# Two transformer blocks with experts on one core: overflow code laid aside, first routing and tail reordered, shorter reciprocal root

## The chip, the core and the metric

The kernel is one program on one core of a Trainium2 chip. The metric is device time in microseconds (us), the median of three runs. Its engines are TensorE (PE), VectorE (DVE), ScalarE (ACT), GpSimd (POOL) and SyncE (SP), each with its own queue of instructions; they wait for one another on semaphores.

## The reference, cut

All tensors are fp32. There are 256 tokens (272 with 16 meta tokens in the first block) of width 1024. The first block has two layers with mixers (a recurrent RG-LRU, then gated linear attention), a layer norm behind each mixer and each feed-forward part, and in its second layer a choice of 2 of 8 experts (width 3584). The second block has a modulated norm, attention, and 2 of 4 experts in the best of 4 groups (16 experts, width 512).

```
h = layer_norm(alpha * h + gla_block(h), g1, b1)              # "ln2" in the kernel
top_w = softmax(top_k(h @ router, 2))                         # routing 1, 8 experts
y = sum_e gates[:, e] * (silu(h @ w_gate[e]) * (h @ w_up[e])) @ w_out[e]
h = layer_norm(alpha * h + y, g2, b2)[16:]                    # "ln3"
x = h + g1 * attention(modulate(rms(h)))                      # the middle
gate = hierarchical top-2 of 16 of x7 = modulate(rms(x))      # routing 2
out = x + g2 * sum_e gate[:, e] * (silu(x7 @ w_g[e]) * (x7 @ w_u[e])) @ w_d[e]
```

## The kernel before

A value that enters a product is split into a high and a low part. In the mixers, the dense feed-forward part and the middle, weights come as a stream `M` of chunks: SyncE loads `raw`, ScalarE makes the high part `whi` (`split_hi`), VectorE the low part `wlo` (`split_lo`), TensorE uses both. For the first chunk of the middle GpSimd makes `wlo` (`pool_split_lo`), and GpSimd also ends the norm `ln3` (`pool_ln`).

*First expert layer.* VectorE's `dve_route1` takes the two largest logits of each token (`dve_top2`), their shares and gates (`dve_top2_gates`) and one-hot `masks`. TensorE multiplies these into counts and ranks. `dve_places` sorts the eight experts by their counts into a list `perm`, which SyncE reads to issue the weights' transfers (`load_first`, a ring R1 of 11 slots of 1.05 MB), and computes for every token its place in its experts' groups (`of_place`) and a flag, whether an expert has more tokens than its pair has room for. The experts work in four pairs, rank x with rank 7-x, in `pe_first`, `act_first` and `dve_first`: `choose` writes the selection matrices `sel`, `choose_sel` turns them, `part` gathers the tokens, `up`, `down` and `scatter` follow. Before `choose(0)`, VectorE also ends the norm `ln2` (`dve_ln_finish`) and makes the tokens' low parts `hl`.

*Overflow.* After each expert layer every engine waits for the others' `round_m1` or `round_m2`, reads the flag from memory and branches over the code of the overflow rounds that stands there in an `If` (`first_again`, `pairs_again`). In the given data the flags are zero. SyncE's output (`sp_out`) stands before its own second `If`.

*The middle.* ScalarE spreads the gate of the attention branch over the partitions (`act_spread`), VectorE and ScalarE make the rms norm, with `gc`, the product of gain and modulation. Reciprocal roots are `dve_rsqrt`: an initial value from the bits and three Newton steps, eleven dependent steps in all.

*Second expert layer.* Eight pairs in `pe_pairs`, `act_pairs` and `dve_pairs`, weights in a ring R2 of 13 slots, issued by `load_ring`. The scattered results of all pairs add up in four banks (Y, `ps0` to `ps3`); the result of a down product lies in two D banks. ScalarE copies a D bank times the token's gate to `yh`, VectorE makes the rest `yl`, TensorE scatters both one pair later. Behind the last scatter VectorE multiplies Y by the modulation's gate `g2t` and adds the residual `h`. The order on each engine is the one the code is written in; no scheduler changes it.

## Time and profile before

| | before |
|---|---|
| median of three runs | 1953.35 us (1952.22 to 1957.31) |
| profiled execution, its own time | 1952.21 us |
| its span | 1950.3 us |
| mean granted TensorE clock | 0.962 |
| busy: PE, DVE, ACT, POOL | 1803.6, 609.2, 474.7, 356.6 us |
| read from memory | 579.96 MB |

Busy time is the time in which an engine works on an instruction; register, branch and semaphore instructions don't count. The stages in order are: the first block up to routing 1 (to about 626 us), the first expert layer (to 1498), the middle (to 1709), the second expert layer (to about 1936) and the end. An idle time is given in square brackets with the instruction that ended it.

### The profile page before, as it was taken

What the parts mean: (1) busy time and instruction counts of PE and PEld (TensorE: products, weight loads), DVE (VectorE), ACT (ScalarE), POOL (GpSimd) and SP (SyncE); (2) the same over time, 40 slices, a digit from 0 to 9 for tenths busy, and PEclk for the clock granted to TensorE, in tenths of its full rate; (3) what the DMA queues carried; (4) which work ended last, traced back from release to release, by engine and by line L of the source; (5) the groups of instructions that cost most, each with busy time, mean ns of one, the idle gap of its engine ahead of it and who ended that gap; (6) DMA issues with size and microseconds to landing.
All of it is one profiled execution on the core that took longest, in us unless ns stands there. A gap on an engine that the chain in (4) does not pass through costs nothing.

```text
span 1950.3 us, 26935 instructions
## 1 busy us (share of the span) xinstructions
PE 1803.6 (92%) x11133; PEld 1026.3 (53%) x11133; DVE 609.2 (31%) x1248; ACT 474.7 (24%) x797; POOL 356.6 (18%) x307
## 2 busy tenths in 40 slices
PE   8999999999987899999999999999996887699996
PEld 7987999777965333323332333223232786544442
DVE  6777555338475200100010000000002686500111
ACT  5854434325421110000100000001001564322120
POOL 3000000000000699999920000000000201000000
PEclk9998999998998799999999999999998898799998
DMA  6545666447625999999999999999995640589995
GB/s 191 157 136 200 199 206 216 152 131 249 195 87 196 395 400 386 420 420 420 416 420 420 420 416 418 420 420 419 418 419 218 181 134 31 216 321 420 419 419 232
DMA packets 152744, 582.93 MB, mean 299 GB/s; under 512 B 11673, under 2 KB 77866, under 8 KB 109600
## 3 DMA queue, kind: packets, MB, share of 16 engines
q1 hardware_dynamic: 150000, 575.09, 75.8%
q0 software_dynamic: 2608, 5.97, 1.2%
q8 instruction: 93, 1.52, 0.3%
q14 instruction: 43, 0.35, 0.1%
HBM read 579.96 MB, written 1.05 MB: 298 GB/s over the span
## 4 chain that ended last, share of the span: by engine, by line
PE 44%; DMA 14%; DVE 6%; ACT 2%; issue 1%; DVEq 0%; SPq 0%; ACTq 0%
PE ps L1765 16%; DMA ring<-in_moe_w_out 10%; PE ps L2200 6%; PE ps L1758 4%; PE ps L1797 4%; PE ps L2224 3%; DMA ring<-in_moe_w_in 3%; PE ps L1801 1%; DMA more<-in_moe_w_in 1%; PE ps L2167 1%; PE ps L2185 1%; PE ps L436 1%; PE ps L2168 1%; PE ps L438 1%; PE ps L437 1%
## 5 line engine op out<-in xcount | busy, mean ns | idle before, releaser
L1765 PE MATMUL ps<-ring,xg 128*64 128x512 f32 x1638 | 407.2, 600 | 5.5 <-DMA ring<-in_moe_w_in 2.6
L472 DVE TENSOR_TENSOR wlo<-raw,whi 128x2048 fp32r<-128x2048 f32 (+5 forms) x96 | 211.5, 2206 | 190.6 <-ACT whi L464 190.3
L1765 PEld LDWEIGHTS ps<-ring,xg 128*64 128x64 f32 x1638 | 121.4, 137 | 249.1 <-issue 239.9
L464 ACT ACTIVATE whi<-raw 128x2048 fp32r<-128x2048 f32 (+6 forms) x97 | 178.8, 1846 | 187.2 <-PE ps L438 70.9
L436 PE MATMUL ps<-xh,whi 128*128 128x272 f32 (+1 forms) x712 | 210.4, 295 | 1.2 <-DVE xl L521 1.2
L438 PE MATMUL ps<-xh,wlo 128*128 128x272 f32 (+1 forms) x712 | 208.5, 293 | 0.0
L1797 PE MATMUL ps<-ring,ahm 128*64 128x512 f32 x808 | 202.9, 597 | 5.9 <-DMA ring<-in_moe_w_out 5.8
L437 PE MATMUL ps<-xl,whi 128*128 128x272 f32 (+1 forms) x712 | 208.3, 293 | 0.0
L2133 POOL TENSOR_SCALAR lnt<-lnt,h 128x384 f32<-128x384 f32 x120 | 188.5, 1571 | 12.2
L1935 DVE TENSOR_TENSOR sgm<-sgm,ps 128x512 f32<-128x512 f32 x28 | 17.4, 682 | 501.1 <-PE ps L1765 501.1
L742 POOL DMA_DIRECT2D lnt<-in_ln_gain x4 | 2.2, 559 | 799.7 <-issue 513.8
L436 PEld LDWEIGHTS ps<-xh,whi 128*128 128x128 f32 (+1 forms) x712 | 133.5, 188 | 4.5 <-issue 2.4
L437 PEld LDWEIGHTS ps<-xl,whi 128*128 128x128 f32 (+1 forms) x712 | 133.7, 188 | 0.4
L438 PEld LDWEIGHTS ps<-xh,wlo 128*128 128x128 f32 (+1 forms) x712 | 133.3, 187 | 0.5
L1797 PEld LDWEIGHTS ps<-ring,ahm 128*64 128x64 f32 x808 | 63.3, 136 | 129.0 <-issue 129.0
L2135 POOL TENSOR_TENSOR bias<-bias,lnt 128x384 f32<-128x384 f32 x120 | 120.2, 1002 | 10.0
L436 PE MATMUL ps<-whi,xh 128*128 128x256 f32 (+3 forms) x368 | 111.7, 304 | 4.2 <-DVE wlo L472 2.0
L437 PE MATMUL ps<-wlo,xh 128*128 128x256 f32 (+3 forms) x368 | 110.6, 301 | 0.0
L438 PE MATMUL ps<-whi,xl 128*128 128x256 f32 (+3 forms) x368 | 110.3, 300 | 0.0
L1758 PE MATMUL ps<-ring,xg 128*32 128x384 f32 (+1 forms) x936 | 106.6, 554 | 2.1 <-DMA ring<-in_moe_w_in 1.9
L2200 PE MATMUL ps<-ring,xg 128*64 128x512 f32 x392 | 99.3, 604 | 1.6 <-ACT xg L2265 1.6
L1945 DVE SCALAR_TENSOR_TENSOR yl<-ps,gs,yh 128x512 fp32r<-128x512 f32 x8 | 5.6, 747 | 265.3 <-ACT yh L1883 265.3
(581 smaller groups left out, 2422.9 us busy)
## 6 DMA issues: line engine op xcount, KB each, us to landing
ring<-in_moe_w_in SPq DMA_DIRECT2D x117, 1024.0 KB, 19.6
ring<-in_moe_w_out SPq DMA_DIRECT2D x101, 1024.0 KB, 19.9
ring<-in_moe_w_in SPq DMA_DIRECT2D x117, 768.0 KB, 11.8
ring<-in_w_gate SPq DMA_DIRECT2D x29, 1024.0 KB, 13.6
raw<-in_ffn_w_in SPq DMA_DIRECT2D x28, 1024.0 KB
ring<-in_w_down SPq DMA_DIRECT2D x26, 1024.0 KB, 13.0
raw<-in_w_ada SPq DMA_DIRECT2D x24, 1024.0 KB
ring<-in_w_up SPq DMA_DIRECT2D x20, 1024.0 KB, 11.9
```

The lines of the kernel that those rows point to most:

```text
L436: e.matmul(o, lh, rh, start=start, stop=False)
L437: e.matmul(o, lh, rl, start=False, stop=False)
L438: return e.matmul(o, ll, rh, start=False, stop=stop)
L464: e.activation(whi[0:rows, s % NSPL, 0:n], raw[0:rows, i % NRAW, 0:n], ACT.Copy).then_inc(S.hi.s, S.hi.up((s,)))
L472: e.tensor_tensor(wlo[0:rows, s % NSPL, 0:n], raw[0:rows, i % NRAW, 0:n], whi[0:rows, s % NSPL, 0:n].bitcast(F32), ALU.subtract).then_inc( ...
L1758: ins = e.matmul(po[32 * c:32 * c + 32, 0:n // 4], a[:, j, 128:160], quarter(both[0][:, 0, :], n, c), start=j == 0, stop=j == 7)
L1765: ins = e.matmul(ps_[b][64 * v:64 * v + 64, :], a[:, j, 64 * v:64 * v + 64], both[v][:, 0, 512 * b:512 * b + 512], start=j == 0, stop=j == 7)
L1797: ins = e.matmul(D[q][64 * v:64 * v + 64, :], w["ahm"][:, f, 64 * v:64 * v + 64], both[v][:, i, 512 * q:512 * q + 512], start=f == 0, stop ...
L2133: e.tensor_scalar(stp[:, :], rel[:, :], float(th), dl[:, i, hh:hh + 1], ALU.is_ge, ALU.mult).then_inc(pool.s, pool.up())
L2135: e.tensor_tensor(bias[:, hh, :], bias[:, hh, :], stp[:, :], ALU.add).then_inc(pool.s, pool.up())
L2200: ins = e.matmul(p[64 * v:64 * v + 64, :], xg[:, kk_, u + 64 * v:u + 64 * v + 64], both[v][:, k, :], start=kk_ == 0, stop=kk_ == 7)
L2224: ins = e.matmul(D[q][64 * v:64 * v + 64, :], w["ah"][:, x % 2, f, 64 * v:64 * v + 64], both[v][:, i, 512 * q:512 * q + 512], start=f == 0 ...
```

## The change

- `dve_rsqrt` keeps three Newton steps, but half of the value is folded into the first two instructions and each step runs on y and x*y*y/2 in two dependent instructions: eight dependent steps.
- Overflow: each compute engine has the overflow rounds' code ahead of its main program (`aside`), jumped over at the start. The flag is loaded into a register earlier (`load_flag`: at step 20 of the first pair of layer 1, and in the second layer at a step of the fifth pair), and at the old place a compare-and-branch (`ask`) falls through where the flag is zero. SyncE has a block of its own for each layer (`sp_first_again`, `sp_pairs_again`), the second now before the output.
- The first chunks of the middle are issued each when the slot of R1 that it overlays is read for the last time (`last_in`), and the parameters of the norms as soon as their buffer is free.
- Routing 1: the masks come before the shares, the counts get a product of their own ahead of the ranks', the sort is `dve_order`, the expert of rank x is paired with the one of rank 4+x (the step `back` goes), the norm's ending and `hh`/`hl` are done per tile, the gather of tile 0 comes before `choose_sel(0)`, and the second tile's part, the shares and the flag (`dve_route1_end`) stand between `choose(0)` and `choose(1)`.
- Start of the middle: the first chunk's low part is made by VectorE in two halves (`split_half`), one before and one after the mean square; ScalarE makes two high parts before its squares.
- Routing 2: masks before the shares.
- Second layer: VectorE multiplies D by gate and `g2t` into `z`, which gives back the D bank; ScalarE copies `z` to `yh`, VectorE makes `yl = z - yh`; the last pair has buffers of its own (`yh7`, `yl7`). The residual is added by a product of the identity with `h` into Y at `scatter(2)`; `scatter(6)` stands behind `down(7)`; the result is copied out of Y half by ScalarE and half by VectorE, and each tile goes out by itself.

```diff
+    def split_half(e, S, s, half):
+        i = S.split[s]
+        a = slice(CW // 2 * half, CW // 2 * half + CW // 2)
+        e.wait_ge(S.hi.s, S.hi.at(s))
+        ins = e.tensor_tensor(wlo[:, s % NSPL, a], raw[:, i % NRAW, a], whi[:, s % NSPL, a].bitcast(F32), ALU.subtract)
+        if half:
+            ins.then_inc(S.lo.s, S.lo.up((s,)))
+        else:
+            ins.then_inc(dve.s, dve.up())
...
+        for i in range(begin, end):
             _, rows, n, pieces, s, zero = S.chunks[i]
             k = i % NRAW
+            if first <= i < first + NRAW:
+                e.wait_ge(pe.s, pe.at("ring", R1.name, last_in(ring[:, 2 * NSPL + k, :])))
             if i >= NRAW:
...
         e.wait_ge(dve.s, dve.n)
-        e.tensor_scalar(y.bitcast(I32), x.bitcast(I32), 1, None, ALU.logical_shift_right).then_inc(dve.s, dve.up())
-        e.wait_ge(dve.s, dve.n)
-        e.tensor_scalar(y.bitcast(I32), y.bitcast(I32), -1.0, 1597463007.0, ALU.mult, ALU.add).then_inc(dve.s, dve.up())
-        e.tensor_scalar(x, x, -0.5, None, ALU.mult).then_inc(dve.s, dve.up())
-        for _ in range(3):
+        e.tensor_scalar(y.bitcast(I32), x.bitcast(I32), -0.5, 1597463007.0, ALU.mult, ALU.add).then_inc(dve.s, dve.up())
+        e.wait_ge(dve.s, dve.n)
+        e.scalar_tensor_tensor(x, y, 0.5, x, ALU.mult, ALU.mult).then_inc(dve.s, dve.up())
+        for i in range(3):
             e.wait_ge(dve.s, dve.n)
-            e.tensor_tensor(tmp, y, y, ALU.mult).then_inc(dve.s, dve.up())
+            e.scalar_tensor_tensor(tmp, x, -1.0, y, ALU.mult, ALU.mult).then_inc(dve.s, dve.up())
             e.wait_ge(dve.s, dve.n)
-            e.tensor_tensor(tmp, tmp, x, ALU.mult).then_inc(dve.s, dve.up())
-            e.wait_ge(dve.s, dve.n)
-            ins = e.scalar_tensor_tensor(y, tmp, 1.5, y, ALU.add, ALU.mult)
-            ins.then_inc(dve.s, dve.up())
+            if i < 2:
+                e.scalar_tensor_tensor(x, tmp, 1.5, x, ALU.add, ALU.mult).then_inc(dve.s, dve.up())
+            e.scalar_tensor_tensor(y, tmp, 1.5, y, ALU.add, ALU.mult).then_inc(dve.s, dve.up())
...
+    def dve_places(e):
+        p = bank("rank", 8)
+        e.wait_ge(pe.s, pe.at("rank", 8))
+        e.tensor_copy(w1["rk"][:, :, 0:8], p[:, 0:32].rearrange("p (t n) -> p t n", t=2)[:, :, 0:8]).then_inc(dve.s, dve.up(("flag", 8)))
+        pick_out(e, of_place[:, 1], masks[:, :, 0:8], 2)
+        pick_out(e, of_place[:, 0], w1["rk"][:, :, 0:8], 2)
         dve.label(("places",))
-        pick_out(back.unsqueeze(1), many.unsqueeze(1), 1)
...
             sel = w["sel"][:, x % 2]
             p, pg = bk.take(e, key, "sel", x), bk.take(e, key, "gs", x)
             e.wait_ge(C.dve.s, C.dve.at(key, "sel", x))
-            e.wait_ge(dve.s, dve.at("places"))
...
 
-        choose_sel(0)
+        e.wait_ge(dve.s, dve.at("m1", "hl"))
+        e.wait_ge(C.dve.s, C.dve.at(key, "sel", 0))
         for i in range(4):
             part(0, i)
+        choose_sel(0)
...
+            return
+        root[engine] = nc.cur_bb
+        e.br(f"{engine}_main")
+        for n, body in bodies:
+            with nc.body(f"{engine}_again{n}", valid_engines=[e.engine]):
+                body(e, engine)
+                e.br(f"{engine}_past{n}")
+        nc.switch_bb(f"{engine}_main")
...
+        e.br_ne(flag[engine, n], 0, on_true=f"{engine}_again{n}", on_false=f"{engine}_past{n}")
+        nc.switch_bb(f"{engine}_past{n}", parent=root[engine])
 
...
         e.wait_ge(dve.s, dve.n)
         e.tensor_copy(tw[:, :, 0:2], gi[:, :, 0:2]).then_inc(dve.s, dve.up())
         e.tensor_tensor(tw[:, :, 2:3], gw[:, :, 41:42], gw[:, :, 40:41], ALU.subtract).then_inc(dve.s, dve.up((key, "gap")))
+        e.wait_ge(dve.s, dve.n)
+        for t in range(2):
+            e.tensor_scalar(masks[:, t, 0:n], io, tw[:, t, 0:1], None, ALU.is_equal).then_inc(dve.s, dve.up())
+            e.tensor_scalar(other[:, t, 0:n], io, tw[:, t, 1:2], None, ALU.is_equal).then_inc(dve.s, dve.up())
...
+        e.wait_ge(dve.s, dve.at("ln2", "full", 0))
+        act_moe_parts(e, "m1", lambda t: w1["hh"][:, t, :], lambda t: h[:, t, :], (0,))
         act_ada(e, 5)
-        e.wait_ge(dve.s, dve.at("ln2", "full"))
-        act_moe_parts(e, "m1", lambda t: w1["hh"][:, t, :], lambda t: h[:, t, :])
+        e.wait_ge(dve.s, dve.at("ln2", "full", 1))
+        act_moe_parts(e, "m1", lambda t: w1["hh"][:, t, :], lambda t: h[:, t, :], (1,))
...
+        e.tensor_scalar(far[:, :], cst[:, C_IO:C_IO + 128], 256.0, None, ALU.add).then_inc(dve.s, dve.up())
+        dve_ln_finish(e, "ln2", 2, XTILES[:1])
         e.wait_ge(pe.s, pe.at("m1", "logits"))
         e.tensor_copy(gw[:, :, 0:8], logits("m1", 8)).then_inc(dve.s, dve.up(("m1", "logits")))
         dve_top2(e, "m1", 0, 8)
+        dve_moe_parts(e, "m1", lambda t: w1["hh"][:, t, :], lambda t: w1["hl"][:, t, :], lambda t: h[:, t, :], (0,))
+        dve_order(e)
+        dve_places(e)
+        e.wait_ge(dve.s, dve.n)
+
+    def dve_route1_end(e):
+        dve_ln_finish(e, "ln2", 2, XTILES[1:])
+        dve_top2_share(e, "m1")
         dve_top2_gates(e, "m1", 8)
-        dve_places(e)
+        dve_moe_parts(e, "m1", lambda t: w1["hh"][:, t, :], lambda t: w1["hl"][:, t, :], lambda t: h[:, t, :], (1,))
+        pick_out(e, of_place[:, 2], gates[:, :, 0:8], 2)
+        dve.label(("gates", "of place"))
         dve_ada(e, 5)
-        dve_ln_finish(e, "ln2", 2, XTILES)
-        e.wait_ge(dve.s, dve.n)
-        dve_moe_parts(e, "m1", lambda t: w1["hh"][:, t, :], lambda t: w1["hl"][:, t, :], lambda t: h[:, t, :])
+        dve_over(e)
 
...
         def scatter(x):
+            if x == 2:
+                for t in range(2):
+                    for q in range(2):
+                        e.matmul(Y[t, q][:, :], idn, h[:, t, 512 * q:512 * q + 512], start=False, stop=False)
             e.wait_ge(C.dve.s, C.dve.at(key, "yl", x, 1))
             for t in range(2):
                 for q in range(2):
-                    for n in ("yh", "yl"):
-                        ins = e.matmul(Y[t, q][:, :], w["selT"][:, x % 3, t, :], w[n][:, 512 * q:512 * q + 512],
-                                       start=(x == 0 and n == "yh"), stop=(x == NP - 1 and n == "yl"))
-            ins.then_inc(C.pe.s, C.pe.up((key, "scat", x)))
+                    for i, y in enumerate(y_of(w, x)):
+                        ins = e.matmul(Y[t, q][:, :], w["selT"][:, x % 3, t, :], y[:, 512 * q:512 * q + 512],
+                                       start=(x == 0 and i == 0), stop=(x == NP - 1 and i == 1))
+                ins.then_inc(C.pe.s, C.pe.up((key, "scat", x), (key, "scat", x, t)))
...
                 up(x + 1, x - 1)
-            else:
-                scatter(x - 1)
             down(x)
+        scatter(NP - 2)
...
-            e.wait_ge(C.pe.s, C.pe.at(key, "D", x))
-            if x:
+            if 0 < x < NP - 1:
                 e.wait_ge(C.pe.s, C.pe.at(key, "scat", x - 1))
-            e.wait_ge(C.act.s, C.act.at(key, "gs", x))
             for q in range(2):
-                e.activation(w["yh"][:, 512 * q:512 * q + 512], bk(key, "D", x, q)[:, :], ACT.Copy,
-                             scale=w["gs"][:, x % 3:x % 3 + 1]).then_inc(C.act.s, C.act.up((key, "yh", x, q)))
+                o = slice(512 * q, 512 * q + 512)
+                e.wait_ge(C.dve.s, C.dve.at(key, "z", x, q))
+                e.activation(y_of(w, x)[0][:, o], w["z"][:, o], ACT.Copy).then_inc(C.act.s, C.act.up((key, "yh", x, q)))
 
...
+            for q in range(2):
+                o = slice(512 * q, 512 * q + 512)
+                if x:
+                    e.wait_ge(C.dve.s, C.dve.at(key, "yl", x - 1, q))
+                e.scalar_tensor_tensor(w["z"][:, o], bk(key, "D", x, q)[:, :], w["gs"][:, x % 3:x % 3 + 1], g2t[:, o],
+                                       ALU.mult, ALU.mult).then_inc(C.dve.s, C.dve.up((key, "z", x, q)))
+            yh, yl = y_of(w, x)
+            if 0 < x < NP - 1:
+                e.wait_ge(C.pe.s, C.pe.at(key, "scat", x - 1))
             for q in range(2):
                 o = slice(512 * q, 512 * q + 512)
                 e.wait_ge(C.act.s, C.act.at(key, "yh", x, q))
-                e.scalar_tensor_tensor(w["yl"][:, o], bk(key, "D", x, q)[:, :], w["gs"][:, x % 3:x % 3 + 1],
-                                       w["yh"][:, o].bitcast(F32), ALU.mult, ALU.subtract).then_inc(C.dve.s, C.dve.up((key, "yl", x, q)))
+                e.tensor_tensor(yl[:, o], w["z"][:, o], yh[:, o].bitcast(F32), ALU.subtract).then_inc(
+                    C.dve.s, C.dve.up((key, "yl", x, q)))
 
         choose(0)
...
             if x + 1 < NP:
                 up(x + 1)
             down(x)
-        e.wait_ge(C.pe.s, C.pe.at(key, "scat", NP - 1))
         for t in range(2):
-            for q in range(2):
-                a = slice(512 * q, 512 * q + 512)
-                e.tensor_tensor(w["y"][:, t, a], bk(key, "Y", t, q)[:, :], g2t[:, a], ALU.mult).then_inc(C.dve.s, C.dve.up((key, "out")))
-            e.wait_ge(C.dve.s, C.dve.n)
-            e.tensor_tensor(h[:, t, :], h[:, t, :], w["y"][:, t, :], ALU.add).then_inc(C.dve.s, C.dve.up((key, "result", t)))
...
         e.wait_ge(pool.s, pool.at("bias"))
         act_spread(e, "g1", g1t)
-        split_hi(e, M, s)
+        for i in range(2):
+            split_hi(e, M, s + i)
         act_mean_sq(e)
-        split_hi(e, M, s + 1)
         act_shift_turn(e, "x5", QTILES, xh, gain_x2, shift_x2, tmpT)
...
         e.scalar_tensor_tensor(gc[:, 1, :], modc[:, 32:40], 1.0, colB[:, 0:8], ALU.add, ALU.mult).then_inc(dve.s, dve.up())
+        split_half(e, M, s, 0)
         dve_mean_sq(e)
+        split_half(e, M, s, 1)
         dve_shift_turn(e, "x5", QTILES, xh, xl, gain_x2, shift_x2, tmpT)
         for i in (1, 2):
...
-        first_again(e, "sp")
+        sp_first_again(e)
         load_chunks(e, M, first, len(M.chunks))
         load_ring(e, second, SLOTS, True)
+        sp_pairs_again(e)
         sp_out(e)
-        pairs_again(e, "sp")
```

The order of instructions at three places follows; a row is line, operation, tiles and shape. VectorE from the end of the sort's use to the first selections of pair 0 in routing 1: the flag (`cnt`, `flags`), column 5 of the modulation (`modc`), the norm's ending (`h<-h,lnt`), the low part `hl`, then `sel`. Before:

```order
L1627 TENSOR_REDUCE srt<-prod 128x8
L1639 TENSOR_SCALAR srt<-srt 128x4 x2
L1641 TENSOR_REDUCE cnt<-srt 128x1
L1643 TENSOR_SCALAR flags<-cnt 128x1
L621 TENSOR_TENSOR modc<-ps,colA 128x2x4
L749 TENSOR_TENSOR h<-h,lnt 128x1024 x2
L753 TENSOR_TENSOR h<-h,lnt 128x1024 x2
L1989 TENSOR_TENSOR hl<-h,hh 128x1024 x2
L1907 TENSOR_SCALAR sel<-cst,of_place 128x64 x2
```

And now, from `perm` on:

```order
L1639 CAST perm<-srt 128x8
L1651 COPY rk<-ps 128x2x8
L1643 TENSOR_TENSOR prod<-masks,pick 128x128
L1646 TENSOR_REDUCE of_place<-prod 128x16
L1643 TENSOR_TENSOR prod<-rk,pick 128x128
L1646 TENSOR_REDUCE of_place<-prod 128x16
L1934 TENSOR_SCALAR sel<-cst,of_place 128x64 x2
L1934 TENSOR_SCALAR sel<-cst,of_place 128x32 x4
L1934 TENSOR_SCALAR sel<-cst,of_place 128x64 x2
L1934 TENSOR_SCALAR sel<-cst,of_place 128x32 x4
L755 TENSOR_TENSOR h<-h,lnt 128x1024
L759 TENSOR_TENSOR h<-h,lnt 128x1024
```

The selections of pair 0 stand before the ending of the second tile, and the first tile's ending and low part stand before `perm`; flag, `modc` and the second `hl` have moved behind.

ScalarE from the branch at the end of the first expert layer to the first shift of the middle (`kk` and `h<-ps` are the spread of the gate, `whi` high parts, L2435 or L2528 the squares). Before:

```order
L1964 UNCONDITIONAL_BRANCH
L2628 ACTIVATE kk<-cst,modc 128x128 x8
L2622 ACTIVATE h<-ps 128x512 x2
L464 ACTIVATE whi<-raw 128x2048
L2435 ACTIVATE hn,rs<-h 128x1024 x2
L2438 ACTIVATE hn<-h,rs 128x1024
L464 ACTIVATE whi<-raw 128x2048
L534 ACTIVATE sq<-ps,modc,gc 128x256
```

And now:

```order
L2045 COMPARE_AND_BRANCH
L2721 ACTIVATE kk<-cst,modc 128x128 x8
L2715 ACTIVATE h<-ps 128x512 x2
L462 ACTIVATE whi<-raw 128x2048 x2
L2528 ACTIVATE hn,rs<-h 128x1024 x2
L2531 ACTIVATE hn<-h,rs 128x1024
L542 ACTIVATE sq<-ps,modc,gc 128x256
```

The unconditional branch over the overflow code is a compare-and-branch, and the second high part has moved ahead of the squares.

TensorE at the end of the second expert layer: the last down product (`ah` times `more`, `xslot` and `ring`, banks `ps6` and `ps7`), the down product before it (`ps4`, `ps7`) and the scatter of pair 6 (L2185, now L2279, into `ps0` to `ps3`). Before:

```order
L2224 MATMUL ps4<-ring,ah_5 64x512
L2224 MATMUL ps4<-more_5,ah_5 64x512
L2185 MATMUL ps0<-yh_5,selT_5 128x512
L2185 MATMUL ps0<-yl_5,selT_5 128x512
L2185 MATMUL ps1<-yh_5,selT_5 128x512
L2185 MATMUL ps1<-yl_5,selT_5 128x512
L2185 MATMUL ps2<-yh_5,selT_5 128x512
L2185 MATMUL ps2<-yl_5,selT_5 128x512
L2185 MATMUL ps3<-yh_5,selT_5 128x512
L2185 MATMUL ps3<-yl_5,selT_5 128x512
L2224 MATMUL ps6<-more_5,ah_5 64x512
L2224 MATMUL ps6<-xslot,ah_5 64x512
```

And now:

```order
L2318 MATMUL ps4<-xslot,ah_5 64x512
L2318 MATMUL ps4<-ring,ah_5 64x512
L2318 MATMUL ps6<-ring,ah_5 64x512 x2
L2318 MATMUL ps7<-ring,ah_5 64x512 x2
L2318 MATMUL ps6<-ring,ah_5 64x512 x2
L2318 MATMUL ps7<-ring,ah_5 64x512 x2
L2318 MATMUL ps6<-ring,ah_5 64x512 x2
L2318 MATMUL ps7<-ring,ah_5 64x512 x2
L2318 MATMUL ps6<-ring,ah_5 64x512 x2
L2318 MATMUL ps7<-ring,ah_5 64x512 x2
L2279 MATMUL ps0<-yh_5,selT_5 128x512
L2279 MATMUL ps0<-yl_5,selT_5 128x512
```

The scatter of pair 6 has moved from ahead of the last down product to behind it.

## Rows read from the trace of the kernel before

**Rows 1.** Table by stage: stretch, busy per engine, clock, DMA share, GB/s

```profile
626.00:1498.00 872.00, 827.89 (x4604) 269.80 (x4604) 66.59 (x173) 56.41 (x111) 315.82 (x248) 0.98 0.99 405
1498.00:1709.00 211.00, 157.09 (x1020) 141.41 (x1020) 142.93 (x367) 102.94 (x229) 17.61 (x21) 0.85 0.44 145
1709.00:1936.00 227.00, 221.44 (x1150) 96.59 (x1150) 21.88 (x48) 45.06 (x105) 0.00 (x0) 0.99 0.94 384
```

**Rows 2.** Timeline, routing 1: start, us, line, op, tiles, [idle before <-releaser]

```profile
623.41 0.17 DVE L1606 SCALAR_TENSOR_TENSOR srt<-ps,cst 128x8 f32<-128x8 f32 x1 [1.42 <-PE ps L1527]
...
625.46 0.17 DVE L1631 CAST perm<-srt 128x8 int32<-128x8 f32 x1
...
626.66 6.26 SPq L1583 DMA_DIRECT2D ring<-in_moe_w_in  x10
...
628.73 2.35 DVE L749 TENSOR_TENSOR h<-h,lnt 128x1024 f32<-128x1024 f32 x2
...
636.94 5.17 DVE L1907 TENSOR_SCALAR sel<-cst,of_place 128x64 fp32r<-128x64 f32 x24
...
639.82 1.08 PE L1657 MATMUL ps<-cst,sel 128*128 128x128 f32 x4 [15.60 <-DVE sel L1907]
...
649.61 6.02 PE L1765 MATMUL ps<-ring,xg 128*64 128x512 f32 x16 [0.79 <-DVE h L2121]
...
656.82 5.27 SPq L1583 DMA_DIRECT2D ring<-in_moe_w_in  x4
```

**Rows 3.** Table by stretch, as rows 1: first layer, second layer's end

```profile
626.00:656.00 30.00, 15.39 (x80) 10.44 (x84) 19.79 (x85) 5.70 (x9) 7.73 (x9) 0.53 0.93 362
...
720.00:750.00 30.00, 29.12 (x175) 10.39 (x178) 3.08 (x5) 2.99 (x6) 27.94 (x23) 1.00 0.90 337
...
750.00:800.00 50.00, 50.00 (x297) 16.16 (x291) 6.76 (x16) 3.92 (x8) 46.67 (x37) 1.00 1.01 418
...
1925.00:1930.00 5.00, 5.00 (x22) 2.42 (x24) 0.00 (x0) 0.00 (x0) 0.00 (x0) 1.00 0.19 79
```

**Rows 4.** Chain that ended last: start, us, what; DVEq is VectorE's sequencer

```profile
1498.53 0.55 DVEq L1964
...
1499.50 3.13 issue
```

**Rows 5.** Timeline, columns as rows 2, the seam to the middle

```profile
1505.85 0.17 DVE L567 TENSOR_SCALAR rs<-rs 128x2 int32<-128x2 int32 x1
...
1507.57 0.60 ACT L2622 ACTIVATE h<-ps 128x512 f32<-128x512 f32 x1 [1.05 <-PE ps L2615]
...
1507.97 2.47 DVE L2919 SCALAR_TENSOR_TENSOR h<-h,mv,lnt 128x1024 f32<-128x1024 f32 x2
...
1512.13 5.08 POOL L2415 TENSOR_TENSOR wlo<-raw,whi 128x2048 fp32r<-128x2048 f32 x1 [10.93 <-ACT whi L464]
...
1512.75 4.48 DVE L2926 SCALAR_TENSOR_TENSOR gc<-modc,colA 128x8 f32<-128x8 f32 x1
...
1519.78 1.15 ACT L2438 ACTIVATE hn<-h,rs 128x1024 f32<-128x1024 f32 x1 [5.65 <-DVE rs L577]
...
1520.84 1.89 ACT L464 ACTIVATE whi<-raw 128x2048 fp32r<-128x2048 f32 x1
```

**Rows 6.** Groups of line 567, the roots written to `rs`, with count

```profile
L567 DVE TENSOR_SCALAR rs<-rs x14: 152/170/285, 155.5 to 1678.5; 128x1 int32<-128x1 int32 x6, 128x2 int32<-128x2 int32 x4, 128x4 int32<-128x4 int32 x2, 128x32 int32<-128x32 int32 x1
```

**Rows 7.** Timeline, columns as rows 2, full fp32 products

```profile
1673.80 1.95 PE L2615 MATMUL ps<-kk,ones 128*128 128x128 f32 x16
```

**Rows 8.** Timeline, columns as rows 2, the last down product and end

```profile
1924.94 0.50 PE L2185 MATMUL ps<-yh,selT 128*128 128x512 f32 x1 [2.23 <-DVE yl L2339]
...
1927.00 7.09 PE L2224 MATMUL ps<-ring,ah 128*64 128x512 f32 x32
...
1942.67 1.23 DVE L2355 TENSOR_TENSOR h<-h,y 128x1024 f32<-128x1024 f32 x1
```

**Rows 9.** Waits of SyncE: line, releaser, us in total

```profile
SPq L2362 <- DMA out<-h: 2.5, 1, 2.5
```

265 lines of the change are left out of this document (146 added, 119 removed).

## The prediction

> **What bounds the kernel now.** I read a table by stage first, then at each seam the order of time on the engines that wait. [rows 1] splits the profiled execution (span 1950.3 us, own time 1952.21): in the first expert layer the DMA share is 0.99, so the transfers set its pace; the middle (attention) has TensorE busy 157.09 of 211 us at a clock of 0.85 of full speed, with work handed from engine to engine; in the second expert layer TensorE is busy 221.44 of 227 us; and 14 us follow until the span's end, with only the last scatter on TensorE. The stage before 626 us is mostly TensorE work and is touched only in its reciprocal roots. So a saving counts at a seam, where nothing covers it, and is read from the first layer's transfers, from the middle's chain and from the second layer's TensorE.
>
> **Term 1, reciprocal roots.** One root runs from 1505.85 to the next instruction at 1507.97, 2.12 us for eleven dependent steps, so 0.193 us a step [rows 5]. The new form has eight; two of them carry a second instruction (about 0.08 us, as the pair in the old form does), so 8 x 0.193 + 0.16 = 1.70, a saving of 0.42 us a root. There are 17 roots: the 14 of [rows 6] and one each written to three other tiles. In the first part of the kernel the first root of each layer norm is hidden by TensorE's products for the next tile; one per norm and one in the linear attention stay on the path: 4 x 0.42 = 1.7. In the middle two stand at its start (in term 3) and six more later: 6 x 0.42 = 2.5, of which I take 2.4, since the two that close the middle overlap TensorE a little. Bounds for the six: 0 and 2.5.
>
> **Term 2, the first routing and the first layer's end.** Three times matter: when the list of experts (`perm`) exists, when TensorE starts, and what the transfers do with both.
> The list: now the sort begins at 623.41 and the cast to `perm` at 625.46 [rows 2]. In the new order the masks come before the shares, only two products (the counts) precede the sort, and one step of the sort is gone. Step by step from the copy of the logits: largest values and indices as before, masks 0.8 us earlier, the low part of tile 0 (half of the 2.4 us that the pair takes) covers the count products, sort at 621.95, cast at 623.6. So `perm` and the first weight transfer come 1.9 us earlier.
> TensorE: now the 15.6 us wait before its first selection product at 639.82 is filled on VectorE by the places, the overflow flag, two tiles of the norm's ending (2.35 for two multiplications at 628.73, as much for the two additions), both low parts and all 24 selection instructions (5.17 us) [rows 2]. In the new order only the places of two kinds, 12 selection instructions (2.6), the second tile's ending (2.35), the shares (1.75) and one low part (1.2) lie between `perm` and the gather: 623.8 + 1.4 + 2.6 + 2.35 + 1.75 + 1.2 = 633.1. From the first selection product (639.82) to the first expert product (649.61) TensorE's preparation takes 9.8 us [rows 2]; 0.8 of it is ScalarE's copy of the last gathered part, which the transposes now cover because they stand behind the gather. So the first expert product can start at 633.1 + 9.0 = 642.1 instead of 649.61: 7.5 us earlier.
> The transfers: eleven slots are issued from 626.66, and the next transfer waits until 656.82 [rows 2], though eleven slots of 1.05 MB need 27.6 us at 418 GB/s, so that some 1.3 us of the 30 stand idle; and from 720 to 750 us they move 337 GB/s where 418 is the level right after [rows 3]: 30 x (1 - 337/418) = 5.8 us idle. Both stops are slots that TensorE had not emptied. If nothing stopped them, the layer would end 1.9 + 1.3 + 5.8 = 9.0 us earlier; if TensorE's start sets them, 7.5. I take 7.5, since the stop at 750 is measured from TensorE's side; the bounds are 5.5 (TensorE 2 us later than worked out) and 9.0. TensorE now also reads the overflow flag inside this layer, at step 20 of the first pair, in the stretch of the stop. VectorE's read takes 0.55 us [rows 4]; TensorE's isn't shown, the bounds are 0 (its queue covers it) and twice VectorE's. I take 0.5. Term 2 is 7.0.
>
> **Term 3, the seam to the middle.** After the last addition of the first layer (1498.32) VectorE reads the flag (0.55), branches, and then stands 3.13 us [rows 4] until the next instruction at 1502.63. The overflow code lies between, and the branch jumps over it. In the new order the code lies ahead of the main program, the flag is already in a register, and the branch falls through: I leave 0.3 of 4.3, a gain of 4.0. The four first weight transfers, which began after this seam, now begin as the last slots empty, and the norm's parameters are loaded long before, so neither comes late in its place.
> Then ScalarE is the next late one. Its spread of the gate ends 5.8 us after its start (1502.36 to 1508.17, the two copies from 1507.57 [rows 5]), now 1504.3, and it then makes two high parts (1.9 each, as the one at 1520.84) before the squares: 1508.2, where VectorE is ready at 1507.1. Squares of both tiles take 2.5, to 1510.7. VectorE meanwhile has its small `gc` step. That took 4.48 us at 1512.75, inside GpSimd's 5.08 us subtraction from 1512.13 [rows 5]; with GpSimd's work gone it takes 0.15, and the first half of the low part (1.15, half of a whole one) fits before 1510.7. The root ends at 1512.65 instead of 1519.78, 7.1 us earlier. The second half (1.15) falls in the 1.2 us in which VectorE waited for the transposes. The high part at 1520.84, which stood in front of ScalarE's shifts, is gone from there: 0.5 more. Term 3 is 7.6, of which 4.0 is the branch; bounds 3.6 and 9.3 (the latter if the spread finds the full clock).
> The Trainium skill (Runtime: NRT & Kernel Launch, Instruction fetch mechanics) says that fetching ahead is sequential and that a taken branch to a target outside the window waits for a fetch. The 3.13 us agree, and no run here shows a branch that falls through. By that rule the new unconditional jump to the end of the program could cost such a fetch again, which is in the first rival.
>
> **Term 4, the second routing.** The masks move ahead of the exponential, but VectorE's own chain to the ranks keeps its length except for the wait on ScalarE: 0.3.
>
> **Term 5, the second layer.** The residual is now added by four full fp32 products of 512 columns in TensorE's stream. Sixteen records of 128 columns (eight products) take 1.95 us at full clock [rows 7]; four products of 512 columns are twice as much, 3.9, with the start of the group; back to back 3.5. Nothing covers it: cost 3.5. TensorE's flag read there: 0.6, bounds as above. In return the scatter of the seventh pair goes behind the last down product. Now that product starts at 1927.00, 4.3 us after the one before it ended (about 1922.7; 2.23 us of wait, then the scatter) [rows 8]. It will wait only for a bank that the first multiplication by the gate gives back, 0.85: gain 3.45. From 1925 to 1930 us the transfers still move 79 GB/s x 5 us = 0.4 MB [rows 3], so the last weights landed near 1926; the product's second half needs them at 1930.4 in the new order, so the transfers don't hold it. Term 5 costs 0.65.
>
> **Term 6, the end.** The last down product ends at 1934.09 [rows 8]. Now the scatter follows 2.2 us later, as it does before it (2.23 [rows 8]), and after it four multiplications by the gate and two additions end at 1942.67 + 1.23 = 1943.90. In the new order two multiplications (0.7 each), two copies and two subtractions (0.57 each) interlock: the scatter starts after 2.75 us, runs tile by tile, and two copies of 0.65 follow: 5.65 after the last down product instead of 9.8, a gain of 4.2. Then the output lands (SyncE waits 2.5 us [rows 9]) near 1946.6, and 3.7 us pass to the end of the span: flag, branch and fetch as at the first seam. They go before the output now; I leave 0.6, a gain of 3.1. Term 6 is 7.3; bounds 3.5 and 8.
>
> **The sum.** 1.7 + 7.0 + 7.6 + 2.4 + 0.3 - 0.65 + 7.3 = 25.65. From the profiled execution's 1952.21 this gives 1926.6, and from the median of the three runs, 1953.35, which lies 1.1 above it, 1927.7.
>
> **Rivals.**
> *The fetch stays*: the compare-and-branch stops the instruction stream even when it falls through, or the jump to the end does. For it: no row shows either. Price 3.1 us at the seam and 3.1 at the end: 1933.9. Against: the 3.13 us [rows 4] come after a jump over a whole overflow round, and nothing else there explains them. Chance 0.15.
> *The transfers stop elsewhere*: the first layer gains only the 1.9 us of `perm`, since slots fill at another place. 5.6 less: 1933.3. Chance 0.12.
> *All bounds good*: the transfers never stop (1.6 more), the spread finds the full clock (1.7): 1924.4. Chance 0.10.
> *Small*: the middle's chain is covered by TensorE work so that its roots and part of term 3 bring nothing, with one of the other rivals; a gain under 5.9 us: chance 0.03.
> *Slower*: the register reads on TensorE empty its queue in both expert layers and the clock falls to its lower level (1.2 GHz). After the 15.6 us gap before 639.82 the mean clock from 626 to 656 is 0.53 [rows 3]. A stretch of 30 us of dense products at half clock costs 15 us, twice that is 30, with 2 us of stop at each read 34, against a sum of 25.65: 1961.7. It decides when a read stops TensorE for several us, not for 0.5. Against it: VectorE's read is 0.55. Chance 0.02.
>
> **How the numbers follow.** The forecast has 0.58 and gives the predicted time, 1927.7; with the terms' own bounds it lies between 1924 and 1932, since their ends don't all fall to one side. The range reaches to the fetch and transfer rivals with some spread, and to the good bound: 1921.5 to 1936. A measurement can tell 0.3%, 5.9 us: faster by more has all but the last two cases, 0.95; within 0.03; slower 0.02.
>
> **What the profile will show.** Right: `perm` within 2 us before 624 less term 1's 1.7; first expert product near 640; no stretch under 400 GB/s between 700 and 760; VectorE's next instruction within 0.5 us of the first layer's last addition; no `gc` over 0.3 us; a root of about 1.7 us; four products of 3.5 us in all in the second layer; output issued some 5.7 us after the last down product. Wrong: idle of about 3 us behind a branch, a transfer rate under 400 at another place in the first layer, or ScalarE's high parts holding the squares for more than 1.5 us.

## The result, and the profile after

| | before | changed |
|---|---|---|
| median, us | 1953.89 (4 runs) | 1938.91 (4 runs) |
| lowest to highest | 1952.22 to 1957.31 | 1937.34 to 1942.90 |
| profiled run: own time, span | 1952.21, 1950.3 | 1938.98, 1936.9 |
| mean granted clock in the profile | 0.962 | 0.964 |

The ratio is 0.9924, with a 95% interval from 0.9904 to 0.9944: faster by 0.8%, and slower than the forecast of 1927.7 by 11.2 us, outside the range (1921.5 to 1936.0). One of the ten executions of the variant `before_roots` ran at a mean granted clock of 0.55 and took 3040 us; it is left out of that variant's median and ratio. The spans of the two profiled executions differ by 13.4 us where the sum said 25.65. Cut at the same events in both traces, with the gain that each stretch gave:

| stretch | before, us | after, us | gain | forecast |
|---|---|---|---|---|
| start to the first product of the first projection | 15.29 | 16.48 | -1.2 | 0 |
| from there to `perm` | 610.17 | 607.27 | +2.9 | +3.6 |
| `perm` to last product of the first expert layer | 860.12 | 859.04 | +1.1 | +5.1 |
| to the middle's first product | 38.73 | 30.85 | +7.9 | +7.6 |
| to the first scores of the attention | 83.60 | 80.54 | +3.1 | +2.4 |
| to the attention's last value | 42.30 | 48.52 | **-6.2** | 0 |
| to the second layer's first product | 59.26 | 59.66 | -0.4 | +0.3 |
| to the start of the last down product | 217.53 | 218.27 | -0.7 | -0.65 |
| to VectorE's last instruction | 16.90 | 12.85 | +4.1 | +4.2 |
| to the end of the span | 6.43 | 3.41 | +3.0 | +3.1 |

The lower half of this table is the forecast almost term by term. Three rows hold most of the miss: the start, the first expert layer and the attention. The table compares one trace of each kernel. How far other traces of the same code lie from these is said with the experiments and at the end of the account.

By stage, the changed kernel (a table of stretches as [rows 1, 3]: busy time of TensorE's products, of its weight loads, VectorE, ScalarE and GpSimd, then clock, DMA share, GB/s):

```profile
624.00:1496.00 872.00, 827.43 (x4604) 269.46 (x4604) 65.47 (x181) 56.22 (x112) 317.17 (x250) 0.99 1.00 411
1496.00:1702.00 206.00, 162.97 (x1020) 147.35 (x1020) 136.84 (x349) 103.10 (x229) 11.14 (x18) 0.83 0.37 123
1702.00:1934.00 232.00, 227.70 (x1166) 100.14 (x1166) 34.01 (x66) 45.96 (x106) 0.00 (x0) 0.99 0.92 377
720.00:750.00 30.00, 29.12 (x178) 10.20 (x176) 3.08 (x5) 2.56 (x5) 27.96 (x22) 1.00 1.02 411
```

The stretch from 720 to 750 us, which moved 337 GB/s [rows 3], is full, as forecast. The timeline of the first routing, the changed kernel (columns as in [rows 2]):

```profile
623.75 0.17 DVE L1639 CAST perm<-srt 128x8 int32<-128x8 f32 x1
...
624.96 6.21 SPq L1601 DMA_DIRECT2D ring<-in_moe_w_in  x10
...
633.15 0.50 PE L1700 MATMUL ps<-sel,hh 128*128 128x160 f32 x1 [9.88 <-DVE hl L2056]
...
641.92 5.31 PE L1789 MATMUL ps<-ring,xg 128*64 128x512 f32 x16
```

The first expert product stands at 641.92 against 649.61 before [rows 2]; the text said 642.1. The lead over the kernel before in the weights' bytes moved is then 8 us from 760 to 900 us of the span. At 1000 us it is 4.8, at 1200 4.1, at 1450 3.5, and at the layer's last product 2.8: what was won at the layer's start was lost inside it.

The seam to the middle, the changed kernel (timeline, columns as in [rows 5]):

```profile
1495.78 0.17 DVE L2999 MEMSET ones<- 128x128 f32 x1 [0.26 <-DVE h L1945]
...
1505.40 0.16 DVE L3019 SCALAR_TENSOR_TENSOR gc<-modc,colA 128x8 f32<-128x8 f32 x1
...
1507.40 0.17 DVE L575 TENSOR_SCALAR rs<-rs 128x2 int32<-128x2 int32 x1
...
1509.12 0.75 DVE L2538 TENSOR_SCALAR hn<-h,rs 128x1024 f32<-128x1024 f32 x1
```

VectorE goes on 0.26 us after the last addition, where it took 4.31 before [rows 4]. `gc` takes 0.16 us where it took 4.48 [rows 5]; nothing of GpSimd runs beside it now. The Trainium skill (SBUF — State Buffer, Who interferes with whom) says that a VectorE instruction with two inputs in SBUF contends with a GpSimd instruction that reads SBUF, and that the ports which the two share are held exclusively. The two numbers agree. A root takes 1.72 us (1507.40 to 1509.12); the text said 1.70 against the 2.12 of [rows 5].

### The profile page after: what moved, and what is told of

Its sections match the earlier page's. It is cut to its first block, busy times and chain, and to the rows that moved or that the text cites. A ratio compares the mean times of both kernels' runs of the same rounds, so it can differ in the third digit from the quotient of the medians.

```text
span 1936.9 us, 26926 instructions
## 1 busy us (share of the span) xinstructions
PE 1812.8 (94%) x11141; PEld 1033.9 (53%) x11141; DVE 607.6 (31%) x1227; ACT 476.9 (25%) x799; POOL 351.6 (18%) x306
## 3 DMA queue, kind: packets, MB, share of 16 engines
HBM read 579.96 MB, written 1.05 MB: 300 GB/s over the span
## 4 chain that ended last, share of the span: by engine, by line
PE 73%; DMA 14%; DVE 8%; ACT 3%; issue 1%; SPq 0%; ACTq 0%; DVEq 0%
PE ps L1789 17%; DMA ring<-in_moe_w_out 9%; PE ps L437 9%; PE ps L438 8%; PE ps L439 8%; PE ps L2294 6%; PE ps L1782 5%; PE ps L1821 4%; PE ps L2318 3%; DMA ring<-in_moe_w_in 3%; DVE wlo L480 2%; DMA more<-in_moe_w_out 1%; PE ps L1825 1%; DMA more<-in_moe_w_in 1%; PE ps L637 1%
## 5 line engine op out<-in xcount | busy, mean ns | idle before, releaser
L2219 POOL TENSOR_SCALAR lnt<-lnt,h 128x384 f32<-128x384 f32 x120 | 188.6, 1572 | 12.2
## 6 DMA issues: line engine op xcount, KB each, us to landing
ring<-in_w_gate SPq DMA_DIRECT2D x29, 1024.0 KB, 14.2
```

Of the source, the lines that this page charges most:

```text
L2219: e.tensor_scalar(stp[:, :], rel[:, :], float(th), dl[:, i, hh:hh + 1], ALU.is_ge, ALU.mult).then_inc(pool.s, pool.up())
```

## Experiments

Times of different chips are not compared closely: each variant's ratio is against the kernel before on its own chip. The changed kernel was measured again (`after_again`) on the chip that `all_three`, `all_three_pause` and `before_params_early` also ran on:

> The changed kernel once more, beside the variants on one chip. Its first profile had the list of experts at 623.75 us, five variants that share the code up to there at 621.4 to 621.9 and one at 625.31. Theory A: this is a spread of the part before routing 1 from one execution to another (where the clock's steps fall between 495 and 585 us), so a second profile lies between 621 and 626, and the first expert layer from the list's cast to the last product takes 858.5 to 859.5 again (first profile 859.04). The attention from the first scores to the first probabilities takes 20.4 us with the clock low for 17 us, as in five of eight profiles of this order, or 18.8 or 17.1 as in three; the median lies at 1934 to 1939 us.

Measured: 1935.86 us (1932.25 to 1937.60, 6 runs), 0.9892 of before [0.9872, 0.9912]. Its span is 1934.7: `perm` to the layer's end 857.67 (859.04 in the first trace), the attention 48.51 again (48.52), the start 17.29. From the first projection's first product to `perm` the twelve traces of the changed order took 603.0 to 608.4 us, so I compare stretches and not spans. The single edits' ratios to the kernel before (0.9875 to 0.9901) all lie within the interval of `after_again`: no single edit shows a difference in the time, and what follows is read from traces, mostly one of each variant.

**1. The norm's parameters.** Two lines of the changed kernel's timeline and the transfers of 975 to 1005 us (queue: packets, MB, share of 16 engines):

```profile
983.97 0.62 POOL L748 DMA_DIRECT2D lnt<-in_ln_gain  x1 [0.56 <-POOL bias L2221]
984.58 0.55 POOL L749 DMA_DIRECT2D lnt<-in_ln_bias  x1
```

```profile
q1 hardware_dynamic: 1706, 11.53, 92.7%
q0 software_dynamic: 288, 1.05, 8.7%
```

The gain and bias of the third norm, 1.05 MB, were fetched at the seam, where few transfers run; GpSimd now fetches them as soon as its biases are made, in the middle of the layer whose pace the transfers set. `params_late` puts them back:

```diff
-        pool_ln(e, 3, (dve, "dl"), (pool, "bias"))
+        pool_ln(e, 3, (dve, "dl"), (pool, "bias"), (pe, "ring", R1.name, len(R1.chunks) - 2))
```

> The changed kernel, but the gain and bias of ln3 (1.05 MB over GpSimd's queue) are issued only when TensorE uses the last but one slot of the first expert layer's ring, and no longer in the middle of that layer near 950 us. Theory A: in the changed kernel these bytes take 1.05 MB / 0.42 MB per us = 2.5 us from transfers that set the pace, so TensorE's lead over the kernel before falls by that much between 950 and 1000 us; now the last expert product of the layer starts 2.5 us earlier (near 1480.3 instead of 1482.79) and the total falls by about 2.5, as long as the parameters land before VectorE needs them some 15 us later. Rival B: the lead is lost because the ring of slots fills, whatever else is moved; then the last product stays at 1482.8 within 0.5 us and the time doesn't change.

The fetch of the gain goes to 1483.03 (timeline of this variant):

```profile
1483.03 0.62 POOL L748 DMA_DIRECT2D lnt<-in_ln_gain  x1 [501.73 <-PE ps L1821]
```

`perm` to the layer's last product is 856.88, against 857.6 to 859.0 in the executions with the early fetch (mean 858.5): 1.6 less; the two joined variants below, also with the late fetch, took 855.8 and 855.6. Between 950 and 1000 us of the span the changed kernel's lead in weight bytes falls by 2.6 us, and in `params_late` by 0.1. From the layer's last product to VectorE's `ones` it is then 14.5 us against 13.0 in the first trace, after a step of the clock at the layer's end; but `after_again` shows 14.5 too, so that isn't this edit's doing. The time is 1934.62, 0.9884 of before [0.9858, 0.9911]. The opposite edit, `before_params_early`, moves the fetch in the kernel before.

```diff
     def pool_mid(e):
-        pool_ln(e, 3, (dve, "dl"), (pool, "bias"))
...
         pool_rel(e)
+        pool_ln(e, 3, (dve, "dl"), (pool, "bias"))
         first_again(e, "pool")
```

> The kernel before, but with the parameters of ln3 loaded where the changed kernel loads them, in the middle of the first expert layer, once GpSimd's last use of their buffer is over. Theory A: 1.05 MB at 0.42 MB per us more in the stretch in which the transfers set the pace: from the list of experts to the layer's last product 862.5 us instead of 860.12, and nothing comes back at the seam, since the parameters weren't late there: 2.4 us slower in the trace. Rival B: no change there, if the slots, not the bytes, hold the layer.

The layer takes 863.00 instead of 860.12, 2.9 more; two other variants that leave the parameters late in the old order (below) took 860.7 and 861.8, so 1.2 to 2.9 more. The bytes are clearer: this trace is 0.3 us behind the kernel before in weight bytes at 950 us of the span and 2.8 at 1000, and keeps that. 1.05 MB at the 418 GB/s of [rows 3] is 2.5 us. This is the first part of the miss. The time is 1962.31 (10 runs), 1.0033 of before [1.0015, 1.0051], 2.9 to 10 us slower; in this trace two pieces of the seam are longer as well, by 2.5 and 1.8 us, at a lower clock, which theory A did not have.

**2. The middle's first weights** also come into the layer's end. `first_chunks_late` holds them back:

```diff
-    e.wait_ge(pe.s, pe.at("ring", R1.name, last_in(ring[:, 2 * NSPL + k, :])))
+    e.wait_ge(pe.s, pe.at("ring", R1.name, max(len(R1.chunks) - 2, last_in(ring[:, 2 * NSPL + k, :]))))
```

> The changed kernel, but the middle's first weight chunks are not issued from 1467 us on, as the ring's slots fall free, but all after the use of the last but one slot of the ring (near 1480). Theory A: ahead of that they share the transfers with the last ring loads, and the last product waits for these: the last product starts 0.7 us earlier (the lead over the kernel before is 3.5 us in bytes at 1450 and 2.8 us at the last product), and the seam takes the same time, since the first high part begins at 1501.4, some 20 us later. Total 0.7 lower. Rival B: the transfers are served in order, so nothing changes before 1485 us, and the chunks come late for ScalarE: 0 to 3 us slower.

858.46 in the layer, no change; 1932.88 us. The layer isn't paced by them at its end, so theory A fails. As rival B said, nothing changes before the last product, and the seam doesn't come later either.

**3. What else the layer lost.** Between 250 and 830 us after its first weight transfer the kernel before moved 242.52 MB, the changed one 241.79 and 241.99 (which includes 1.05 MB of parameters), and `params_late` 241.68. The same time moves 0.5 to 0.8 MB less, 1.2 to 1.9 us. Over all traces it is 242.2 to 242.5 MB in the four of the old order and 241.7 to 242.1 in the twelve of the new one, on the means 0.5 MB or 1.1 us less. One thing in which the layers differ is which experts are paired. `old_pairs` restores that:

```diff
-            e.tensor_tensor(..., rank.unsqueeze(1)..., io[:, 4 * u:4 * u + 4]..., ALU.is_equal)
+        e.tensor_scalar(back, rank, -1.0, 7.0, ALU.mult, ALU.add)
+            e.tensor_tensor(..., r.unsqueeze(1)..., io[:, 0:4]..., ALU.is_equal)
```

> The changed kernel, but with the experts paired as before: rank x with rank 7-x. Between 250 and 830 us after the first weight transfer the two queues moved 242.4 to 242.5 MB in three traces of the old pairing and 241.7 to 242.0 in six of the new one, 0.6 MB or 1.4 us less. Theory A: it is the other order of the experts' weights in memory, then 242.4 MB are moved again and the layer's last product comes 1.4 us earlier behind the list of experts (857 us instead of 857.7 to 859.0). Rival B: it comes with the earlier start of TensorE, then the bytes stay at 241.7 to 242.0.

241.92 MB, and 858.31 in the layer; 1937.63 us. The pairing isn't the cause. Neither are the parameters, which `params_late` doesn't load there. It stays open.

**4. The start.** Timeline of before, then of the changed kernel:

```profile
0.83 0.17 DVE L831 MEMSET lnt<- 18x128 f32 x1 [0.83 <-PEq L3239]
...
1.65 0.89 SPq L772 DMA_DIRECT2D h<-in_x  x2
...
7.38 2.75 PE L499 MATMUL ps<-cst,h 16*128 16x16 f32 x10 [7.38 <-DMA h<-in_x]
```

```profile
1.64 2.26 SPq L778 DMA_DIRECT2D h<-in_x  x2
3.75 0.17 DVE L837 MEMSET lnt<- 18x128 f32 x1 [3.75 <-issue]
...
9.13 1.09 PE L507 MATMUL ps<-cst,h 16*128 16x16 f32 x4 [9.13 <-DMA h<-in_x]
```

Each engine that holds laid-aside code first jumps over it. VectorE's first instruction comes 2.9 us later; SyncE, which holds none, needs 2.26 us for the two transfers of `x` instead of 0.89, and TensorE waits for that `x`. `aside_inside` moves the laid-aside code and the jump of ScalarE and VectorE into the first layer (of the two the lines for ScalarE stand here); `aside_all_inside` moves TensorE's too:

```diff
-        aside(e, "act", ((0, first_again), (1, pairs_again)))
...
+        if (x, step) == (0, 20):
+            aside(e, "act", ((0, first_again), (1, pairs_again)))
...
+        aside(e, "pe", ((0, first_again), (1, pairs_again)))
         pe_first(e, main, "m1", w1, load_flag("pe", 0, "m1", (0, 20)))
```

> The changed kernel, but ScalarE and VectorE jump over the overflow code inside the first pair of the first expert layer, where they idle for tens of us, and not at the program's start (TensorE still does it at the start, where it waits for the first transfer until 7 to 9 us anyway). Theory A: at the start the jump costs each of the two 2.8 us (first instruction at 3.57 and 3.75 us instead of 0.74 and 0.83) and with it the first products 1.2 us (16.48 instead of 15.29); moved, these come back: first product at 15.3, total 1.2 us lower. Rival B: the later start is SyncE's (its second transfer of x is issued 1.4 us later) and comes from TensorE's jump or from the length of the program: then ScalarE starts at 0.7 but the first product stays at 16.4.

ScalarE and VectorE start at 0.73 and 0.82 us, but the first projection's first product stays at 16.74: it isn't their jump (1934.57 us).

> The changed kernel, but no engine jumps over the overflow code at the start: ScalarE and VectorE do it in the first pair of the first expert layer, TensorE ahead of its first gather in routing 1, where it waits 9.9 us for VectorE. Moving it for the first two alone brought their first instructions back to 0.7 and 0.8 us, but the first product stayed at 16.7. Theory A: TensorE's jump is behind it: the first product comes back to 15.3, and the total falls by 1.3. Rival B: SyncE's second transfer of x, issued 1.4 us later, is late for another reason (the program's length or its own code): the first product stays at 16.5 to 16.9.

With TensorE's jump gone too (timeline of `aside_all_inside`):

```profile
1.64 0.88 SPq L778 DMA_DIRECT2D h<-in_x  x2
...
7.39 2.75 PE L507 MATMUL ps<-cst,h 16*128 16x16 f32 x10 [7.39 <-DMA h<-in_x]
```

That first product is at 15.11, against 15.29 before the change, and the span 1928.6 (time 1933.63). In the four traces without TensorE's jump at the start (`aside_all_inside`, the two joined variants of point 8 and `inline_rounds`) the first product comes at 14.75 to 15.40 us, in the eight with it at 16.48 to 17.29. So it is TensorE's jump, with the laid-aside code that moves with it, that costs 1.2 to 1.7 us, and it does so through another engine's DMA issue. In the first 4 us the changed kernel moves packets of the queues of kind `instruction` (packets, MB, share):

```profile
q8 instruction: 1, 0.02, 1.9%
q14 instruction: 2, 0.02, 1.8%
```

`aside_inside` has the one of q8, `aside_all_inside` and the kernel before have none. How such a fetch holds up SyncE's issue isn't shown.

**5. The branch.** `inline_rounds` keeps the early reading of the flags but puts the overflow code back in line:

```diff
-        e.br_ne(flag[engine, n], 0, on_true=f"{engine}_again{n}", on_false=f"{engine}_past{n}")
-        nc.switch_bb(f"{engine}_past{n}", parent=root[engine])
+        with e.If(flag[engine, n] != 0):
+            body(e, engine)
```

> The changed kernel with its early reading of the flags, but with the overflow code back in its place behind each expert layer, so that a branch is taken over it where the flag is zero, and nothing is jumped over at the start. Theory A (the instruction fetch behind a taken branch): VectorE stands again some 3 us at the seam (its next instruction 3.3 us behind the last addition instead of 0.26) and some 3 us pass between the last output and the end of the span; the start comes back by 1.2 to 1.5 us (first product at 15.3). Total 4.5 to 5 us slower than the changed kernel. Rival B: the 4 us at the seam were the read of the flag from memory and the waits for the other engines, which are early here too: then the seam stays at 0.3 to 1 us and the total is 1 us faster. Start, rival C: the later first product has nothing to do with the jumps, then it stays at 16.5.

The time is 1935.17, 0.9901 of before [0.9880, 0.9922]: the 4.5 to 5 us of theory A don't show. The branch instructions of the three kernels (engine, operation, times, least/median/most ns, from first to last start): before, then `inline_rounds`, then changed.

```profile
L1964 PEldq COMPARE_BRANCH  x1: 3747/3747/3747, 1499.5 to 1499.5; - x1
```

```profile
L2037 PEldq COMPARE_BRANCH  x2: 3777/3804/3832, 1484.8 to 1923.4; - x2
L2037 DVEq COMPARE_BRANCH  x2: 63/68/72, 1489.8 to 1925.6; - x2
```

```profile
L2045 PEldq COMPARE_BRANCH  x2: 71/86/100, 1489.6 to 1930.6; - x2
L2045 DVEq COMPARE_BRANCH  x2: 43/50/56, 1493.2 to 1932.8; - x2
```

And the chain that ended last, in `inline_rounds`, at this seam (start, us, what):

```profile
1492.15 0.59 issue
...
1492.96 0.18 DVE ones L2991
```

A taken branch costs TensorE's queue 3.8 us and one that falls through 0.1. VectorE's own branch shows 0.07 us, but its next instruction comes 3.1 us behind it (1489.8 to 1492.96), as far as before. Yet VectorE stands idle for only 0.81 us, where it stood 4.31 before: with the flag in a register VectorE's sequencer executes the branch 2.3 us before the last addition ends, and the fetch runs beside the additions. So of the 4.05 us won here, 3.5 belong to the early read and 0.55 to the laid-aside code. At the end of the program, where less work stands between branch and end, laid-aside code gives more: from VectorE's last instruction to the end 3.42 against 5.06 us, 1.65. It costs 1.2 to 1.7 at the start, so in all it gains 0.5 to 1.0 us. The Trainium skill (Runtime: NRT & Kernel Launch, Instruction fetch mechanics) calls a taken branch out of the fetched window a stall; the traces agree, with these numbers.

The fetch stands in the traces among the DMA queues (packets, MB, share of 16 engines), from the first of the last additions to VectorE's next instruction: before, then `inline_rounds`.

```profile
q14 instruction: 3, 0.02, 1.3%
q8 instruction: 1, 0.02, 1.3%
```

```profile
q14 instruction: 1, 0.01, 0.8%
```

Before, these packets start at 1500.0 us, 0.5 behind the branch, while VectorE stands; in `inline_rounds` the packet starts at 1490.9, while the additions run. The changed kernel has none in this stretch. Which engine a packet is for isn't named.

**6. The second layer's residual.** `residual_vector` takes the fp32 products out and lets VectorE add the residual as it copies the result:

```diff
-            if x == 2:
-                ... e.matmul(Y[t, q][:, :], idn, h[:, t, 512 * q:512 * q + 512], start=False, stop=False)
...
-            e.tensor_copy(h[:, t, 512:1024], bk(key, "Y", t, 1)[:, :])
+            for q in range(2):
+                e.tensor_tensor(h[:, t, o], bk(key, "Y", t, q)[:, :], h[:, t, o], ALU.add)
```

> The changed kernel without the four products of the identity with the residual; instead VectorE adds h to all four banks at the end (four additions of 512 columns in place of two copies by ScalarE and two by VectorE). Theory A: TensorE's stream in the second expert layer is shorter by the 3.44 us by which its lead fell there, and the end is longer by one addition more per tile: the second tile's pair ends 0.7 + 0.4 us later. Net 2.3 us faster. Rival B: the product of the residual is covered by a wait for weights or for a bank that then shows: the lead of the later pairs returns to 2.98 us and the total is 1 us slower.

1933.41 us. TensorE reaches the last up products 3.42 us earlier, so the price of [rows 7] was right (the changed kernel's products took 3.70). But then it waits for weights (waits of TensorE: line, releaser, us in total, times, longest):

```profile
PE ps L2314 <- DMA ring<-in_w_down: 2.3, 2, 1.3
```

Of the 2.3 us of theory A only 1.0 arrives at VectorE's last instruction, 1.3 at the end of the span. In the changed kernel TensorE has no such wait in this layer: its longer stream hid the transfers.

**7. The clock in the attention.** Two stretches, from the first scores to the last probabilities, and from there to the last value (columns as in [rows 1]): before, then changed.

```profile
1607.91:1625.04 17.13, 12.99 (x81) 10.17 (x80) 14.46 (x34) 11.80 (x49) 0.00 (x0) 0.80 0.28 111
1625.04:1650.21 25.17, 18.16 (x138) 16.67 (x137) 14.77 (x37) 9.53 (x37) 1.10 (x2) 0.93 0.00 1
```

```profile
1594.18:1614.57 20.39, 16.20 (x84) 13.57 (x83) 14.46 (x34) 14.11 (x58) 0.00 (x0) 0.67 0.23 92
1614.57:1642.70 28.13, 21.20 (x137) 19.54 (x136) 14.91 (x38) 7.43 (x26) 1.10 (x2) 0.82 0.00 1
```

The same lines of the program, VectorE busy for the same time, and a granted clock of 0.67 and 0.82 instead of 0.80 and 0.93. The clock was at its lower level (1.2 GHz) for 17.1 us from 6.8 us behind the first scores, before the change for 6.8 us from 5.7. The attention takes 48.5 us in both traces of the changed kernel, and 42.3 and 42.2 in the two of the old order with the old root (`before`, `before_params_early`). `before_roots` is the kernel before with the new root alone (eight dependent steps for eleven; one of its lines):

```diff
         for _ in range(3):
...
-            e.tensor_tensor(tmp, y, y, ALU.mult).then_inc(dve.s, dve.up())
-            e.wait_ge(dve.s, dve.n)
-            e.tensor_tensor(tmp, tmp, x, ALU.mult).then_inc(dve.s, dve.up())
+            e.scalar_tensor_tensor(tmp, x, -1.0, y, ALU.mult, ALU.mult).then_inc(dve.s, dve.up())
```

> The kernel before with the shorter reciprocal root alone. By the terms on record: 1.7 us in the first part and 0.4 at the seam and 2.4 in the middle, 4.5 us faster. By the two traces: up to the first routing the changed kernel regained only 0.3 us at the first norm and 0.5 at the last, none at the others, so 0.8; the seam and the middle up to the attention 0.8 and 2.5; theory A: 4 us up to the attention's first scores. Rival B (TensorE's clock decides): the attention stage from the first scores on takes 6 us longer than before as in all five traces of the changed order (its granted clock at the lower level for 17 us instead of 7), if being earlier alone moves it there; then the total is the same or 2 us slower.

```profile
1604.22:1624.60 20.38, 16.07 (x84) 13.56 (x83) 14.45 (x35) 14.11 (x58) 0.00 (x0) 0.68 0.24 93
1624.60:1651.56 26.96, 20.03 (x139) 18.30 (x137) 14.89 (x37) 7.43 (x26) 1.10 (x2) 0.86 0.00 1
```

(Windows of `before_roots`.) It leads by 3.7 us at the first scores, loses 5.0 in the attention, and trails by 1.4 at its last value: 1952.66 against 1955.38 us, 0.9979 [0.9960, 0.9999]. So the roots alone are enough to bring a long low stretch, in this trace. `pause_2` then adds two copies that do nothing, 1.42 us of VectorE, to the changed kernel's chain 6 us ahead of the scores:

```diff
+        for _ in range(2):
+            e.wait_ge(dve.s, dve.n)
+            e.tensor_copy(d5[1], d5[1]).then_inc(dve.s, dve.up())
         e.tensor_scalar(rq[:, 1], rd[:, 0], 0.125, None, ALU.mult)
```

> The changed kernel with two needless copies of 128x1024 (about 0.7 us each) in VectorE's chain ahead of the attention's scores, so that everything from there on is some 1.4 us later. Theory A: in five traces of the changed order TensorE's clock falls to its lower level 6.7 to 6.9 us after the first score instruction and stays there for 17.1 us; before it fell 5.7 us after it and stayed 6.8 us. [...] Rival B: the longer stretch belongs to the new order itself: then the lower level lasts 17 us as in the others, and the total is 1.4 us slower.

```profile
1598.56:1615.68 17.12, 10.99 (x75) 8.26 (x75) 14.45 (x34) 12.09 (x50) 0.00 (x0) 0.90 0.29 111
1615.68:1642.79 27.11, 20.19 (x138) 18.71 (x137) 14.94 (x37) 9.07 (x36) 1.27 (x3) 0.81 0.00 1
```

(Windows of `pause_2`.) The stage falls from 48.5 to 44.2 us, and the stretch ahead of it grows by 1.7, so 2.6 stay; 1932.90 us, 0.9881 of before [0.9859, 0.9904]. Work was added on the path, and no loss of time shows. The clock fell 5.7 us behind the scores, as in the kernel before, but for 3.4 us, and later again for 6.8 and 3.4. The joined variants of point 8 make the same pair once more: without the pause the attention takes 48.50 us, with it 42.11, for 1.7 us more ahead of it. The scores' stretch and the whole attention in `all_three_pause`:

```profile
1593.32:1610.42 17.10, 12.39 (x75) 9.22 (x75) 14.46 (x34) 11.76 (x48) 0.00 (x0) 0.80 0.27 111
1593.32:1635.43 42.11, 30.58 (x212) 25.90 (x211) 29.23 (x71) 21.31 (x84) 1.10 (x2) 0.88 0.11 45
```

The same pause in `before_roots`:

> The kernel before with the shorter root, and with the two needless copies ahead of the attention's scores. With the root alone the trace led the kernel before by 3.7 us at the first scores and trailed it by 1.4 us at the last probabilities, the clock being at its lower level for 17 us instead of 7 there. Theory A (where the clock's step falls relative to the scores decides): the fall moves from 7.2 to some 5.7 us behind the first scores, the lower level lasts 7 us, the stage from first scores to first probabilities takes 17.1 us instead of 20.4 and the next 25 to 27 instead of 27, so that the pause of 1.7 us gives back 3.3 to 5 us: 1.6 to 3.3 us faster than with the root alone. Rival B: the clock falls where it falls by chance; then the lower level lasts 17 us again and the trace is 1.7 us longer.

1950.42 us (0.9962 of before [0.9948, 0.9975]), but in the trace the low stretch began 4.4 us behind the scores and lasted 20.5 us. Neither theory had that. This trace can't judge the pause: the low stretch of 6.8 us that `before_roots` has 41 us ahead of the scores is missing in it, and that place comes before the added copies. In the 14 traces whose clock has such an earlier low stretch and is at its full level at the first scores, the place of the fall goes with the length of the attention (times in us):

| traces | fall, behind the first scores | that low stretch | attention |
|---|---|---|---|
| `before`, `before_params_early`, `all_three_pause` | 5.5 to 5.7 | 6.8 | 42.1 to 42.3 |
| `pause_2` | 5.7 | 3.4 | 44.2 |
| `inline_rounds`, `aside_all_inside` | 6.6, 6.7 | 10.2 | 45.4 |
| the changed kernel twice, five variants | 6.8 to 6.9 | 17.1 | 48.5 to 48.8 |
| `before_roots` | 7.2 | 17.1 | 47.4 |

`old_pairs` is the other exception: the clock falls 2.9 us ahead of the scores and again 14.2 behind them (10.2 us low, attention 47.6). The middle's code is the same in rows three and four, and 0.1 us of shift between them goes with 3 us of attention. The pause moved the scores, not the fall: in the table's traces of the changed order it is 80.3 to 80.6 us from the middle's first product to the scores without it and 82.1 to 82.2 with it, to the fall 86.9 to 87.5 and 87.8 to 87.9. So the place of the fall relative to the scores goes with the loss; what sets that place is open.

**8. Together.** `all_three` joins `params_late`, `residual_vector` and `aside_all_inside`; `all_three_pause` adds the pause.

> The changed kernel with three of the edits: the jumps over the overflow code inside the first layer, the parameters of ln3 at the first layer's end, the residual added by VectorE. Singly they gave in the traces 1.3 us at the start, 1.9 us between the list of experts and the last product of the first layer, and 1.0 us in the second layer and the end. Theory A: they add up to 4.2 us against the changed kernel on the same chip, unless the clock's steps change the seam or the attention (up to 1.5 and 3 us either way). Rival B: the first layer's end only hands the time on to a stretch at the lower clock (the seam took 1.5 us longer with the parameters late), then the sum is 2.5.

1929.61 us (1927.42 to 1930.69), 0.9865 of before [0.9844, 0.9887], 6.3 below the changed kernel on the same chip (1932.25 to 1937.60), where theory A said 4.2; the layer takes 855.80, 2.7 less than the mean 858.5, and the start is at 14.75.

> The same with the two needless copies ahead of the attention's scores. Theory A: if without them the clock is low for 17 us in the attention, the pause gives back 4.3 us for 1.4 (net 2.9), and if it is low for 10 us there, it gives nothing (0 to -1.4). Rival B: the place of the clock's steps relative to the attention isn't the same from one execution to another, then the medians of the two differ by the pause alone, 1.4 us.

1927.02 us (1921.62 to 1932.37), 0.9853 [0.9829, 0.9877]: the shortest median, 8.8 below the changed kernel on the same chip; the intervals of the two joined versions overlap, so which of them is the faster isn't shown by the times. In the traces the attention gives back 6.4 us for 1.7, more than theory A's 4.3 for 1.4.

## Why the prediction was wrong, point by point

**Term 1, roots.** The size of a root was right (1.72 for 1.70). The step "one per norm and one in the linear attention stay on the path: 4 x 0.42" was made without looking, norm by norm, at which engine came late there. Between the first two traces the kernel gained 0.3 us at the first norm, 0.5 at the last before the routing and nothing at the others, 0.9 less than the term. But that isn't shown to be a miss: two traces with the old root and the same code to `perm` differ by 1.8 us there (610.2 and 608.4), and over all traces the gain to `perm` is 3.8 us for the forecast 3.6.

**Term 2, the first layer.** The routing was right: the piece behind the last norm up to `perm` is shorter by 2.06 us for 1.9, the first expert product at 641.92 for 642.1, the stop at 720 to 750 us gone. Two steps failed. The first is in term 3: "the norm's parameters are loaded long before", priced at nothing. It is a transfer moved into a stage that I had myself called bound by transfers; `before_params_early` loses 2.5 us of weight bytes between 950 and 1000 us for it, and by its size it is 2.5. The second is that 7.5 us of lead at the layer's start would still be there at its end: 1.2 to 1.9 us (1.1 on the means of all traces) went by a rate that was lower by 0.2 to 0.35%, whose cause the runs didn't settle. The rival "the transfers stop elsewhere" had the sign and the place of this (5.6 less; 4.0 measured), but its mechanism, slots that fill, isn't what happened: the DMA share is 1.00. One bound was also added up wrongly: from 626.66 to 656.82 is 30.2 us, so with 27.6 us of transfers 2.5 stand idle and not 1.3 [rows 2], and the good bound's "1.6 more" is 9.0 - 7.5 = 1.5 by its own terms. Neither touches the forecast.

**A term that was missing, the start.** Moving code to the front of the program has a price at the front: a jump on each engine. The rule of the Trainium skill (Runtime: NRT & Kernel Launch, Instruction fetch mechanics) on taken branches stood beside term 3 and was applied there to the new jump at the end, in the first rival, and not to this one. 1.2 us in the first trace, shown by `aside_all_inside` against `aside_inside`.

**Term 3, the seam.** Right in sum: 7.9 for 7.6 (the seam took 30.9 us in this trace of the changed order and 30.4 to 33.2 in the others). "I leave 0.3 of 4.3, a gain of 4.0" was 4.05. But the reason was half wrong: I put it to the laid-aside code, and `inline_rounds` shows that reading the flag early brings 3.5 of it. The first rival, the fetch stays, is refuted by the 0.1 us of TensorE's branch and the 0.26 us of VectorE.

**The middle.** The roots and term 3's last parts gave 3.1 to the first scores for 2.4; part of it is a higher clock in a stretch there, not the roots. Then the step that failed most: the sum held the attention at its old length. The clock granted in it was 0.80 and 0.93 before, so both levels were in it already, and nothing said that they would keep their places; the same code then had a low stretch of 17.1 us in place of 6.8. -6.2 us, half of the miss. In `before_roots` the roots suffice to bring it; `pause_2` and `all_three_pause` show that 1.4 us more of work in the chain takes 4.3 and 6.4 us of it away. A fall 5.7 us behind the first scores goes with 42 to 44 us, one 6.8 us behind with 48.5. Why the clock falls where it does isn't shown. I had cut the middle into a chain of instructions and read its clock only as an average, in [rows 1].

**Terms 5 and 6.** Right: the four fp32 products took 3.44 us from the lead for 3.5, the reordered scatter gave 3.39 for 3.45; then 4.05 for 4.2 and 3.0 for 3.1. That the sum of term 5 came out (0.7 for 0.65) is luck: the flag's read on TensorE cost nothing for 0.6, and 0.7 us went in the layer's first 6 us, 4.5 of them at the lower clock against 3.1 before.

**The slower rival** had the clock as its mechanism, but in the expert layers, where the reads on TensorE cost nothing and the clock is 0.99.

In sum: 12.2 us of span are missing between the first two traces. 6.2 are the attention's clock, 1.2 the start, 4.0 the first expert layer (2.5 for the parameters, the rest the unexplained transfer rate); what is left is 0.7 ahead of `perm` and about as much behind the attention, less 1.0 won beyond the forecast at the seam and in the middle. The means over all traces in which the edits that bear on a stretch stand as in the kernel before, or as in the changed one, say which of these hold (us, number of traces):

| stretch | before | changed | gain | forecast |
|---|---|---|---|---|
| start to the first projection | 15.4 (4) | 16.8 (8) | -1.4 | 0 |
| from there to `perm` | 609.3 (2) | 605.5 (12) | +3.8 | +3.6 |
| first expert layer | 860.9 (3) | 858.4 (9) | +2.4 | +5.1 |
| attention | 42.2 (2) | 47.8 (10) | -5.6 | 0 |

The start, the layer and the attention stay; the roots don't. By the times, too, part of the first comparison's miss was its own: measured again, the changed kernel takes 1935.86 us against 1956.44 before, 20.6 less for the forecast 25.65.

## What to carry to other kernels

When a change reorders code, list every DMA that it moves and ask what the transfers do at the new place: 1 MB in a stage at DMA share 1.00 costs its bytes, 2.5 us, however small it looks. To take a branch off the path, read its flag early; laying the code aside adds little where work stands in front of the branch, and puts a jump wherever it is laid. A chained stage with a mean clock between the two levels has no fixed length: give it a range of several us whenever anything ahead of it moves. And before a difference of 1 or 2 us between two traces is given a cause, look at how far two traces of the same code lie apart there.

## What the runs showed of the hardware that I had not expected

- A taken branch behind an expert layer costs TensorE's queue 3.7 to 4.3 us (four traces of the old order and `inline_rounds`) and VectorE 3.1 until its next instruction; one that falls through 0.1 and less. A fetch that starts while the engine still has queued work is hidden (0.81 us seen of it).
- A jump on TensorE at the start, with a 16 KB packet of the instruction queue q8, lengthened SyncE's issue of two transfers from 0.89 to 2.26 us; taking the jump off ScalarE and VectorE alone didn't change the first product's time.
- The attention's longest low-clock stretch took one of four lengths over 16 traces: 6.8, 10.2, 17.1 or 20.5 us (4, 3, 8 and 1 of them). With 17.1 us the stage took 48.5 us in six executions (the changed kernel twice, and four variants), 48.8 in a seventh and 47.4 in `before_roots`. A fall of the clock 6.7 or 6.8 us behind the first scores made 3 us of difference in the same code.
